# Seven block products in place of eight for the down projection of three MLP quarters, in a two-layer decoder trunk

## The chip, the cores and the metric

One NeuronCore of a Trainium2 chip runs the whole program in one launch. The metric is the device time of one execution in microseconds (us). The engines are TensorE (PE in the profile; PEld is its weight load), VectorE (DVE), ScalarE (ACT), GpSimd (POOL) and SyncE (SP), which issues the DMAs.

## The reference, cut to what matters

Two layers (DEPTH = 2), SEQ = 512 tokens, D_MODEL = 1024, D_FF = 4096, all in float32. Each layer runs four token mixers side by side, merges and projects them, and then runs the MLP, which is the part that is changed:

```python
hm = rms_norm(x, norm_mlp_pre[l])
u = jax.nn.relu(hm @ w_up[l])
x = x + rms_norm(jnp.square(u) @ w_down[l], norm_mlp_post[l])
```

## The kernel before, in words

Activations lie feature-major: 8 tiles of 128 features by 512 tokens. A float32 product is made of three passes of TensorE over rounded parts. Every operand is split into a high part (fp32r) and a low part (the operand minus its high part), and `product3` issues hi·hi, lo·hi and hi·lo into one bank of PSUM. So every weight has to be split: SyncE loads a chunk of 128x1024 values (512 KB), ScalarE writes its high part (`split_ahead`, L1724, or `hi_part`, L1314), and GpSimd writes its low part by a subtraction in four pieces of 128x256 (`lo_pieces`, L1789), which then counts `w_split` up. TensorE waits for `w_split` before it uses the chunk. There are four slots for chunks and four further slots in the slab.

The MLP goes in four quarters of 1024 hidden features (loop variables `q`, `b`). A quarter has 16 units: 8 "up" units (one tile of 128 hidden features each, from 8 contraction steps), then 8 "down" units (one tile of 128 output features each). A unit is 8 contraction steps times 3 passes, 24 matmuls of 128x512 (the first four units of a layer's MLP and its last four go in two halves of 256 tokens). After an up unit ScalarE takes its bank with relu into `tmp` (L1730), and VectorE squares it (L2448), rounds it into `u_hi` (L2450) and subtracts for `u_lo` (L2452). After a down unit VectorE adds its bank to `acc` (L2457), which GpSimd cleared by a memset (L1813). Unit j uses bank 4 + j % 4.

Each engine works through its own queue in program order, and semaphores tie the queues together. In the down units ScalarE and GpSimd split weights three to four chunks ahead of TensorE (`AHEAD` = 3), as the slots come free. Each engine's order is written out by hand in its block; nothing plans it. The squares of the MLP's input, from which its epsilon term comes, are summed by GpSimd in the last quarter.

Of the kernel before, what the change touches and what calls it, by code (L numbers as in the profile page):

```python
# [60 lines left out]
UNITS = MLP0 + 16 * QUARTERS  # L61
# [12 lines left out]
CHUNKS = MLP_CHUNK0 + 16 * QUARTERS  # L74
# [3 lines left out]
SKIPPED = (MLP_CHUNK0 + 10, MLP_CHUNK0 + 13)  # L78
# [5 lines left out]
def slot_of(c):  # L84

    if c < EXTRA:
        return SLOTS + ENTRY.index(c)
    if 0 <= c - MLP_CHUNK0 < EXTRA:
        return SLOTS + c - MLP_CHUNK0
    return (c - 2 - EXTRA * (c > MLP_CHUNK0) + sum(k <= c for k in SKIPPED)) % SLOTS  # L90

# [4 lines left out]
assert (CHUNKS - 2 * EXTRA + len(SKIPPED)) % SLOTS == 0  # L96
# [176 lines left out]
def trunk_kernel(nc, x_in, wproj, wmerge, wrest, par_in, con_in, mask_in, rope_in, out):  # L273
# [5 lines left out]
    with ctx:  # L279
# [35 lines left out]
        def wload(s_):  # L315
# [17 lines left out]
             for i, n in enumerate(("hi", "lo"))]  # L333
        con = sb("con", [P, NCON])
# [14 lines left out]
        ps = [ctx.enter_context(nc.psum_tensor(f"bank{i}", [P, 512], f32)) for i in range(8)]  # L349

# [74 lines left out]
        w_arrived = [ctx.enter_context(nc.semaphore(f"weights_arrived_{s}")) for s in range(SLOTS + EXTRA)]  # L425
        par_loaded = signal("params_loaded", 32)
# [5 lines left out]
        w_split = signal("weights_split", CHUNKS)  # L432
        act_took = signal("act_took_dense", ACT0)
        dve_took = signal("dve_took_dense", DVE0 + 16 * QUARTERS)
        relu_done = signal("relu_ready", 8 * QUARTERS)
        hid_hi = signal("hidden_hi_ready", 8 * QUARTERS)
        dve_step = signal("dve_step", 176)
# [11 lines left out]
        xsummed = signal("x_squares_added", KT - 1)  # L449
# [112 lines left out]
        acc0 = signal("acc_cleared", 1)  # L562
        u_ready = signal("hidden_ready", 8 * QUARTERS)
# [6 lines left out]
        def _(sp):  # L570
# [31 lines left out]
            for layer in layers():  # L602
# [22 lines left out]
                for j in range(EXTRA, 16):  # L625
                    sp.wait_ge(*dense_done.at(layer, FREED_BY[BEFORE[MLP_CHUNK0 + j]] + 1))
                    load(MLP_CHUNK0 + j, rows(wrest, NREST, KT + j))
                more = layer + 1 < LAYERS
                if more:
                    sp.wait_ge(*dense_done.at(layer, MLP0 + EXTRA))  # L630
                    for c in ENTRY:
                        load(c, rows(wproj, NPROJ, NPROJ + c))
                with sp.Fori(0, QUARTERS - 1) as q:
                    for j in range(16):
                        need = sp.snap(layer * UNITS + q * 16 + (MLP0 + 16 + j - SLOTS + 1))
                        sp.wait_ge(dense_done.handle, need)
                        load(MLP_CHUNK0 + 16 + j, wrest[bass.ds(sp.snap(layer * NREST + q * 16 + (KT + 16 + j)), 1)])
# [11 lines left out]
        def _(pe):  # L649
# [5 lines left out]
            for L in layers():  # L655
# [550 lines left out]
                def unit(q, b, j, k, src, cols=slice(0, T)):  # L1206
                    return product3(ps[4 + j % 4][:, cols], weights(MLP_CHUNK0 + 16 * b + j, k), [v[:, k, cols] for v in src],
                                    k == 0, k == KT - 1)
# [3 lines left out]
                def ready(q, b, j):  # L1212
                    more_split = min(max(j - 8, 0), EXTRA) if more and b == QUARTERS - 1 else 0
                    pe.wait_ge(*w_split.at(L, q * 16 + (MLP_CHUNK0 + 16 * b + j + 1 + more_split)))
                    pe.wait_ge(*dve_took.at(L, q * 16 + (DVE0 + 16 * b + j - 3)))

                def units(q, b, times, j0, j1):

                    for j in range(j0, j1):
                        ready(q, b, j)  # L1220
                        for k in range(KT):
                            if j == 8:
                                pe.wait_ge(*u_ready.at(L, q * 8 + (8 * b + k + 1)))
                            ins = unit(q, b, j, k, hn if j < 8 else u)
                        ins.then_inc(*dense_done.up(times))

                for n in range(2):
                    for pair in range(2):
                        if n == 0:
                            pe.wait_ge(*w_split.at(L, MLP_CHUNK0 + 2 * pair + 2))  # L1230
                        for k in range(KT):
                            if pair == 0:
                                pe.wait_ge(*h_ready.at(L, (2 + n) * KT + k + 1))
                            for j in (2 * pair, 2 * pair + 1):
                                ins = unit(0, 0, j, k, hn, HALF[n])
                                if n == 1 and k == KT - 1:
                                    ins.then_inc(*dense_done.up())
# [5 lines left out]
                units(0, 0, 1, 4, 16)  # L1243
                with pe.Fori(0, QUARTERS - 2) as q:
                    units(q, 1, QUARTERS - 2, 0, 16)
                last = QUARTERS - 1
                units(0, last, 1, 0, 11)
                pe.wait_ge(*xsummed.at(L, KT - 1))
                mm(ps[1][:, :], C("ones"), xsq[:, 0, :]).then_inc(*sumsq.up())
                units(0, last, 1, 11, 12)  # L1250
                for n in range(2):
                    for j in range(12, 16):
                        if n == 0:
                            ready(0, last, j)
                        else:
                            pe.wait_ge(*down_half_took.at(L, j - 11))
                        for k in range(KT):
                            ins = unit(0, last, j, k, u, HALF[n])
# [8 lines left out]
        def _(act):  # L1267
# [42 lines left out]
            for L in layers():  # L1310
# [365 lines left out]
                def enter_mlp(n, m0, m1):  # L1676
                    for m in range(m0, m1):
                        act.wait_ge(*x_tiles.at(L, (2 + n) * KT + m + 1))
                        split_x(m, n, hn[0], "mpre")
# [32 lines left out]
                def square(m, n=None):  # L1712

                    cols = slice(0, T) if n is None else HALF[n]
                    act.wait_ge(*(down_half_took.at(L, m - 3) if n == 0 else dve_took.at(L, DVE0 + 16 * (QUARTERS - 1) + 8 + m + 1)))
# [4 lines left out]
                def split_ahead(q, b, j, times):  # L1720
                    c = MLP_CHUNK0 + 16 * b + j + AHEAD
                    s_ = SLOT[c]
                    act.wait_ge(w_arrived[s_], L * (16 * LOADS[s_]) + q * 64 + 16 * LOADED[c])
                    fn(wchunk(0, s_), wload(s_), ACT.Copy).then_inc(*w_hi_done.up(times))  # L1724

                def relu(q, b, j, times):
                    act.wait_ge(*dense_done.at(L, q * 16 + (MLP0 + 16 * b + j + 1)))
                    if j >= 4:
                        act.wait_ge(*u_ready.at(L, q * KT + (8 * b + j - 3)))
                    fn(tmp[:, j % 4, :], ps[4 + j % 4][:, :], ACT.Relu).then_inc(*relu_done.up(times))  # L1730

                for j in range(16):
                    if j == 7:
                        relu(0, 0, j, 1)
                    if j:
                        split_ahead(0, 0, j, 1)
                    if j < 7:
                        relu(0, 0, j, 1)
                with act.Fori(0, QUARTERS - 2) as q:
                    for j in range(16):  # L1740
                        split_ahead(q, 1, j, QUARTERS - 2)
                        if j < 8:
                            relu(q, 1, j, QUARTERS - 2)
# [8 lines left out]
                for j in range(13):  # L1752
                    split_ahead(0, last, j, 1)
# [4 lines left out]
                    if j < 8:  # L1758
                        relu(0, last, j, 1)
# [23 lines left out]
        def _(pool):  # L1783
            pool.memset(v1st[:, :, :], 0.0).then_inc(cleared, 1)
            for L in layers():
# [25 lines left out]
                pool.wait_ge(*m_split.at(L, KT))  # L1811
                pool.sem_inc(carrier, 1)
                pool.memset(acc[:, :, :], 0.0).then_inc(*acc0.up())  # L1813

                def lo_ahead(q, b, j, times):
                    pool.wait_ge(*w_hi_done.at(L, q * 16 + (MLP_CHUNK0 + 16 * b + j + AHEAD + 2)))
                    lo_pieces(SLOT[(MLP_CHUNK0 + 16 * b + j + AHEAD + 1)]).then_inc(*w_split.up(times))

                for j in range(16):
                    lo_ahead(0, 0, j, 1)  # L1820
                with pool.Fori(0, QUARTERS - 2) as q:
                    for j in range(16):
                        lo_ahead(q, 1, j, QUARTERS - 2)
                more = L + 1 < LAYERS

                def lo_in_turn(turn, c):
                    pool.wait_ge(*w_hi_done.at(L, MLP_CHUNK0 + 16 * (QUARTERS - 1) + turn + 1))
                    lo_pieces(SLOT[c]).then_inc(*w_split.up())

                for j in range(16):  # L1830
# [3 lines left out]
                    if i < 16:  # L1834
                        lo_in_turn(i + (min(max(i - 8, 0), EXTRA) if more else 0), MLP_CHUNK0 + 16 * (QUARTERS - 1) + i)
                    if 8 <= i < 12 and more:
                        lo_in_turn(2 * i - 7, CHUNKS + ENTRY[i - 8])
                    if j < KT - 1:
                        if j:
                            pool.wait_ge(*xsummed.at(L, j))  # L1840
                        pool.tensor_tensor(xsq[:, 0, :], xsq[:, 0, :], xsq[:, j + 1, :], ADD).then_inc(*xsummed.up())

        @block.vector
        def _(dve):
# [34 lines left out]
            for L in layers():  # L1879
# [561 lines left out]
                dve.wait_ge(*acc0.at(L, 1))  # L2441
                carry_wait()

                def hidden(q, b, m, times):

                    r_ = tmp[:, m % 4, :]
                    dve.wait_ge(*relu_done.at(L, q * KT + (8 * b + m + 1)))
                    tt(r_, ps[4 + m % 4][:, :], r_, MUL).then_inc(*dve_took.up(times))  # L2448
                    dve.wait_ge(*dve_took.at(L, q * 16 + (DVE0 + 16 * b + m + 1)))
                    dve.tensor_copy(u[0][:, m, :], r_).then_inc(*hid_hi.up(times))  # L2450
                    dve.wait_ge(*hid_hi.at(L, q * KT + (8 * b + m + 1)))
                    tt(u[1][:, m, :], r_, u[0][:, m, :].bitcast(f32), SUB).then_inc(*u_ready.up(times))  # L2452

                def added_down(q, b, m, times):
# [125 lines left out]
```

## Time and profile before

| what | value |
|---|---|
| runs shown | 1925.84 us median of 3 (1922.8 to 1928.35) |
| the profiled execution | 1926.18 us, span 1924.4 us |
| mean granted TensorE clock | 0.994 |
| HBM read over the span | 155.39 MB |
| one MLP (layer 0), without its ends | about 605 to 950 us of the span |

The span is the time from the first to the last instruction on the core. The busy time of TensorE counts a matmul until its modelled end, while the next one has already begun; so the time that a matmul costs is the distance between two starts, not its own length. For VectorE, ScalarE and GpSimd the length of one instruction is close to what it costs, and it includes the time that the instruction stood waiting for a port.

### The profile page before, as it was taken

The page shows a single profiled execution, that of the slowest core. Times are in us where ns is not written, and L with a number is a line of the kernel's source. Part 1 is how long each engine was busy: PE and PEld are TensorE (multiplying, and loading weights), DVE is VectorE, ACT ScalarE, POOL GpSimd, SP SyncE. Part 2 cuts the span into 40 slices and gives each one's busy share as a digit, 9 for nine tenths or more (in the row PEclk, how much of TensorE's full clock was granted, in tenths as well). Part 3 has the DMA queues.
Part 4 walks back from the last instruction along what each step waited for, and adds up shares of the span by engine and source line. Part 5 has one row for each costly group of instructions (what it writes and reads, how often), then busy time and mean ns, then how long its engine had stood idle before and what let it go on. Part 6 is the DMA issues. An engine that isn't in the chain of part 4 may idle for free.

```text
span 1924.4 us, 32405 instructions
## 1 busy us (share of the span) xinstructions
PE 1891.5 (98%) x13030; PEld 1542.4 (80%) x13030; DVE 975.7 (51%) x1779; ACT 775.2 (40%) x1223; POOL 975.4 (51%) x1195
## 2 busy tenths in 40 slices
PE   9999999999999999999999999999999999999997
PEld 8886867778779888888998777678777898888887
DVE  7957987233435422314588579862434362313154
ACT  7544373235536222223474344722354462222223
POOL 3644524326484655557636444353364845555572
PEclk9999999999999999999999999999999999999999
DMA  5222311112131142222203123111122312222222
GB/s 193 80 88 66 99 44 56 36 56 85 59 134 64 66 153 99 98 95 93 97 30 111 66 77 99 45 43 37 52 92 61 136 45 99 99 98 92 94 99 77
DMA packets 52842, 159.44 MB, mean 83 GB/s; under 512 B 5216, under 2 KB 17632, under 8 KB 52448
## 3 DMA queue, kind: packets, MB, share of 16 engines
q1 hardware_dynamic: 51552, 154.65, 23.9%
q10 hardware_dynamic: 1152, 2.86, 0.4%
q8 instruction: 97, 1.59, 0.3%
q14 instruction: 41, 0.34, 0.1%
HBM read 155.39 MB, written 2.10 MB: 82 GB/s over the span
## 4 chain that ended last, share of the span: by engine, by line
PE 88%; DVE 5%; POOL 3%; ACT 3%; issue 1%; DMA 0%; SPq 0%; DVEq 0%; ACTq 0%
PE bank L660 26%; PE bank L662 24%; PE bank L661 24%; POOL w_lo L1789 2%; PE bank L770 1%; PE bank L1039 1%; PE bank L799 1%; PE bank L999 1%; PE bank L785 1%; PE bank L1051 1%; PE bank L862 1%; POOL wx_lo L1789 1%; POOL slab L1810 1%; DVE slab L2215 1%; PE bank L937 1%
## 5 line engine op out<-in xcount | busy, mean ns | idle before, releaser
L1789 POOL TENSOR_TENSOR w_lo<-w_raw,w_hi 128x256 fp32r<-128x256 f32 x1072 | 837.4, 814 | 916.5 <-ACT w_hi L1314 613.4
L660 PE MATMUL bank<-hn_hi,w_hi 128*128 128x512 f32 x1248 | 513.7, 412 | 0.5 <-DVE tmp L1941 0.3
L662 PE MATMUL bank<-hn_hi,w_lo 128*128 128x512 f32 x1248 | 489.2, 392 | 0.5 <-issue 0.5
L661 PE MATMUL bank<-hn_lo,w_hi 128*128 128x512 f32 x1248 | 489.0, 392 | 0.0
L660 PEld LDWEIGHTS bank<-hn_hi,w_hi 128*128 128x128 f32 x1248 | 235.4, 189 | 68.1 <-issue 20.7
L660 PE MATMUL bank<-u_hi,w_hi 128*128 128x512 f32 (+1 forms) x800 | 287.1, 359 | 1.5 <-DVE u_lo L1952 1.1
L1724 ACT ACTIVATE w_hi<-w_raw 128x1024 fp32r<-128x1024 f32 x120 | 127.4, 1061 | 389.8 <-DMA w_raw<-wrest 389.8
L661 PE MATMUL bank<-u_lo,w_hi 128*128 128x512 f32 (+1 forms) x800 | 284.1, 355 | 0.0
L662 PE MATMUL bank<-u_hi,w_lo 128*128 128x512 f32 (+1 forms) x800 | 284.1, 355 | 0.0
L662 PEld LDWEIGHTS bank<-hn_hi,w_lo 128*128 128x128 f32 x1248 | 235.5, 189 | 51.6 <-issue 1.0
L661 PEld LDWEIGHTS bank<-hn_lo,w_hi 128*128 128x128 f32 x1248 | 236.0, 189 | 47.2 <-issue 4.8
L660 PEld LDWEIGHTS bank<-u_hi,w_hi 128*128 128x128 f32 x800 | 151.0, 189 | 26.8 <-DVE u_lo L1952 2.9
L661 PEld LDWEIGHTS bank<-u_lo,w_hi 128*128 128x128 f32 x800 | 151.1, 189 | 21.5 <-issue 0.5
L662 PEld LDWEIGHTS bank<-u_hi,w_lo 128*128 128x128 f32 x800 | 151.0, 189 | 21.3
L1314 ACT ACTIVATE w_hi<-w_raw 128x1024 fp32r<-128x1024 f32 x148 | 155.5, 1056 | 21.5 <-DMA w_raw<-wmerge 12.9
L2457 DVE TENSOR_TENSOR slab<-slab,bank 128x512 f32<-128x512 f32 x56 | 38.5, 688 | 241.5 <-PE bank L662 241.5
L2448 DVE TENSOR_TENSOR tmp<-bank,tmp 128x512 f32<-128x512 f32 x64 | 44.2, 691 | 181.6 <-ACT tmp L1730 181.6
L1374 ACT ACTIVATE tmp<-bank 128x512 f32<-128x512 f32 x64 | 37.5, 602 | 122.4 <-PE bank L662 122.3
L1810 POOL TENSOR_TENSOR slab<-slab,tmp 128x512 f32<-128x512 f32 x48 | 67.7, 1438 | 3.9 <-DVE tmp L1941 3.9
L1730 ACT ACTIVATE tmp<-bank 128x512 f32<-128x512 f32 x64 | 38.4, 599 | 74.2 <-PE bank L662 74.1
L2452 DVE TENSOR_TENSOR u_lo<-tmp,u_hi 128x512 fp32r<-128x512 f32 x64 | 61.4, 959 | 2.2
L2171 DVE CUSTOM_DVE_ANT_0 slab<-bank,slab 128x256 f32<-128x256 f32 (+3 forms) x56 | 28.4, 517 | 61.2 <-PE bank L777 47.1
(405 smaller groups left out, 2877.0 us busy)
## 6 DMA issues: line engine op xcount, KB each, us to landing
w_raw<-wrest SPq DMA_DIRECT2D x136, 512.0 KB, 3.2
w_raw<-wmerge SPq DMA_DIRECT2D x80, 512.0 KB, 3.5
w_raw<-wproj SPq DMA_DIRECT2D x52, 512.0 KB, 3.2
wx_raw<-wproj SPq DMA_DIRECT2D x4, 512.0 KB, 4.8
wy_raw<-wproj SPq DMA_DIRECT2D x4, 512.0 KB, 7.8
slab<-rope ACTq DMA_DIRECT2D x2, 1024.0 KB, 6.0
wx_raw<-wrest SPq DMA_DIRECT2D x4, 512.0 KB, 5.1
wy_raw<-wrest SPq DMA_DIRECT2D x4, 512.0 KB, 5.6
```

The source lines that it names most:

```text
L660: mm(o_, stat[0], mov[0], start=first, stop=False)
L661: mm(o_, stat[0], mov[1], start=False, stop=False)
L662: return mm(o_, stat[1], mov[0], start=False, stop=last)
L1314: fn(wchunk(0, SLOT[c]), wload(SLOT[c]), ACT.Copy).then_inc(*w_hi_done.up(times))
L1374: ins = fn(tmp[:, i % 4, :], b_, ACT.Sigmoid)
L1724: fn(wchunk(0, s_), wload(s_), ACT.Copy).then_inc(*w_hi_done.up(times))
L1730: fn(tmp[:, j % 4, :], ps[4 + j % 4][:, :], ACT.Relu).then_inc(*relu_done.up(times))
L1789: ins = pool.tensor_tensor(wchunk(1, s_)[:, cs], wload(s_)[:, cs], wchunk(0, s_)[:, cs].bitcast(f32), SUB)
L1810: pool.tensor_tensor(acc[:, m, :], acc[:, m, :], tmp[:, m % 4, :], ADD).then_inc(*merged.up())
L2448: tt(r_, ps[4 + m % 4][:, :], r_, MUL).then_inc(*dve_took.up(times))
L2452: tt(u[1][:, m, :], r_, u[0][:, m, :].bitcast(f32), SUB).then_inc(*u_ready.up(times))
L2457: tt(acc[:, m, :], acc[:, m, :], ps[4 + m % 4][:, :], ADD).then_inc(*dve_took.up(times))
```

## The change

Three of the four quarters of each MLP (q = 0, 1, 2) compute their down projection with Strassen's algorithm. The 1024x1024 block of `w_down` is taken as 2x2 blocks of 512x512 (b11 to b22), the hidden features as two halves of 512 features by two halves of 256 tokens, and seven block products take the place of eight.

- TensorE: each product has two units of 24 matmuls of 128x256, so 14 units follow the 8 up units in a quarter, in the order of `TURN` = 3, 6, 5, 7, 4, 1, 2. Products 1 and 6 stay in banks 0 to 3 over the three quarters; the others go through banks 4 to 7 and are taken out after each.
- SyncE: ten of the 14 weight chunks are sums or differences of two blocks, so each comes with two loads of 512 KB (`load_block`), the second into one of three buffers in the slab. The MLP uses six slots in turn here.
- VectorE: it makes the weights' sums (`weights_sum`, 128x1024), the sums of token parts (`tokens_sum`, 128x1024, five in a quarter), the low parts of the seven token parts (`tokens_lo`, 128x1024) and, for the four chunks of products 5 and 2, which have no sum, the weights' low parts (`weights_lo`, 128x1024). It copies or adds the five products that are not kept (`evicted`, two banks each, 128x512). In these quarters the square is written to `u_raw` and is not split. In the last quarter it combines the products into `acc` (`combine`).
- ScalarE: high parts of 14 chunks and of seven token parts (128x1024 each).
- GpSimd: low parts of the 8 up chunks and of 10 of the 14 down chunks, in pieces as before. The memset of `acc` goes, and the sums of the input's squares move to VectorE, at the start of the MLP.
- The last quarter keeps its eight down units. All loops over quarters are unrolled.

The diff, cut to its core:

```diff
+SEVEN, RUN = QUARTERS - 1, KT + 14
+LASTQ = SEVEN * RUN
+FACTORS = {1: ("b11", "b22", "+"), 2: ("b11",), 3: ("b12", "b22", "-"), 4: ("b21", "b11", "-"), 5: ("b22",),
+           6: ("b11", "b12", "+"), 7: ("b21", "b22", "+")}
+TURN = (3, 6, 5, 7, 4, 1, 2)
+BANKS_OF = {3: (4, 5), 6: (2, 3), 5: (6, 7), 7: (4, 5), 4: (6, 7), 1: (0, 1), 2: (4, 5)}
+BY_VECTOR = (5, 2)
...
+    if p < EXTRA:
+        return SLOTS + p
+    if p < 2 * EXTRA:
+        return p - EXTRA
+    if p < LASTQ:
+        return (SLOTS + 2, SLOTS + 3, 0, 1, 2, 3)[(p - 2 * EXTRA) % 6]
...
 # SyncE
+                for p in range(EXTRA, MLP_UNITS):
+                    c = MLP_CHUNK0 + p
+                    sp.wait_ge(*dense_done.at(layer, FREED_BY[BEFORE[c]] + 1))
+                    if rest_row(p) is not None:
+                        load(c, rows(wrest, NREST, rest_row(p)))
+                    else:
+                        load_block(wload(SLOT[c]), p, 0).then_inc(w_arrived[SLOT[c]], 16)
+                    n = sums_to(p)
+                    if n:
+                        i = (n - 1) % 3
+                        if n > 3:
+                            sp.wait_ge(*w_sum.at(layer, n - 3))
...
+                        load_block(second[i][:, :], p, 1).then_inc(second_arrived[i].handle, 16)
...
 # TensorE
+                def seven_products(q):
+
+                    for k, i in enumerate(TURN):
+                        pe.wait_ge(*t_ready.at(L, parts_ready(q, k)))
+                        tokens_ = comb[(7 * q + k) % 3]
+                        for h in range(2):
+                            p = RUN * q + KT + 2 * k + h
+                            if i not in BY_VECTOR:
+                                pe.wait_ge(*w_split.at(L, MLP_CHUNK0 + split_to_count(p)))
...
+                            for d in range(2):
+                                for f in range(4):
+                                    ins = product3(ps[BANKS_OF[i][h]][:, HALF[d]], weights(MLP_CHUNK0 + p, 4 * d + f),
+                                                   [v[:, f, :] for v in tokens_[0:2]],
...
+                            ins.then_inc(*dense_done.up())
...
 # ScalarE
+                for q in range(SEVEN):
+                    for r in range(RUN):
+                        k = (r - KT) // 2
+                        if r == 4:
+                            tokens_hi(q, 0)
+                            tokens_hi(q, 1)
+                        if r >= KT and r % 2 == 0 and k + 2 < 7:
+                            tokens_hi(q, k + 2)
+                        if (q, r) == (0, 0):
+                            split_mlp(4)
+                        if r < KT:
+                            relu(q, r)
+                        if (q, r) != (0, 0) and RUN * q + r + 4 < LASTQ + 3:
+                            split_mlp(RUN * q + r + 4)
...
 # GpSimd
-                pool.memset(acc[:, :, :], 0.0).then_inc(*acc0.up())
...
+                for p in range(EXTRA, LASTQ + EXTRA):
+                    if not split_by_vector(p):
+                        lo_part(MLP_CHUNK0 + p)
...
 # VectorE
+                dve.wait_ge(*mlp_sq.at(L, 2 * KT))
+                for n in (4, 2, 1):
+                    link(tt(xsq[:, 0:n, :], xsq[:, 0:n, :], xsq[:, n:2 * n, :], ADD), xsummed)
...
+                def weights_sum(p):
...
+                    tt(wload(s_), wload(s_), second[i][:, :], ADD if sign == "+" else SUB).then_inc(*w_sum.up())
...
+                    for m in range(KT):
+                        if m == 0 and q:
+                            evicted(q - 1, 6)
+                        squared(q, m)
+                        if m == 3:
+                            tokens_sum(q, 1)
+                            tokens_lo(q, 0)
+                        if m == 4:
+                            weights_sum(RUN * q + m + 4)
+                            tokens_lo(q, 1)
+                        elif m > 4:
+                            weights_sum(RUN * q + m + 4)
+                        if (q, m) == (0, KT - 1):
+                            eps_term()
+                    for k in range(7):
+                        if k + 2 < 7:
+                            tokens_sum(q, k + 2)
+                        weights_sum(RUN * q + KT + 2 * k + 4)
+                        if k:
+                            evicted(q, k - 1)
+                        if k + 2 < 7:
+                            tokens_lo(q, k + 2)
+                        weights_sum(RUN * q + KT + 2 * k + 5)
+                        for h in range(2):
+                            weights_lo(RUN * q + KT + 2 * k + 4 + h)
+                evicted(SEVEN - 1, 6)
...
+                for m in range(KT):
+                    hidden(m)
+                    if m < 3:
+                        combine(m)
+                for m in range(4):
+                    added_down(m)
```

## Rows read from the trace of the kernel before

**Rows 1.** The page: busy time and share of the span; then the chain that ended last

```profile
PE 1891.5 (98%) x13030; PEld 1542.4 (80%) x13030; DVE 975.7 (51%) x1779; ACT 775.2 (40%) x1223; POOL 975.4 (51%) x1195
...
PE 88%; DVE 5%; POOL 3%; ACT 3%; issue 1%; DMA 0%; SPq 0%; DVEq 0%; ACTq 0%
```

**Rows 2.** Windows: first quarter's down units, then the next quarter's up units

```profile
core 0: us, PE busy (x) PEld busy (x) DVE busy (x) ACT busy (x) POOL busy (x), PEclk, DMA share, GB/s
...
651.00:694.50 43.50, 43.50 (x194) 36.03 (x193) 6.63 (x10) 10.16 (x10) 21.13 (x30) 1.00 0.44 157
694.50:738.00 43.50, 43.50 (x194) 36.03 (x193) 16.20 (x22) 12.64 (x15) 25.25 (x36) 1.00 0.29 97
```

**Rows 3.** Windows: a stretch in which all matmuls are 128x256

```profile
597.00:604.90 7.90, 7.90 (x68) 7.90 (x67) 5.74 (x16) 6.16 (x15) 2.44 (x1) 1.00 0.59 195
```

**Rows 4.** Timeline, GpSimd, first quarter's down units: start, length (us), idle before

```profile
655.62 2.83 POOL L1789 TENSOR_TENSOR w_lo<-w_raw,w_hi 128x256 fp32r<-128x256 f32 x4 [8.09 <-ACT w_hi L1724]
```

**Rows 5.** Groups by line and shape: busy, mean ns of one, idle before

```profile
L1789 POOL TENSOR_TENSOR w_lo<-w_raw,w_hi 128x256 fp32r<-128x256 f32 x1072 | 837.4, 814 | 916.5 <-ACT w_hi L1314 613.4 <-ACT w_hi L1724 302.6
...
L2448 DVE TENSOR_TENSOR tmp<-bank,tmp 128x512 f32<-128x512 f32 x64 | 44.2, 691 | 181.6 <-ACT tmp L1730 181.6
...
L2457 DVE TENSOR_TENSOR slab<-slab,bank 128x512 f32<-128x512 f32 x56 | 38.5, 688 | 241.5 <-PE bank L662 241.5
...
L1724 ACT ACTIVATE w_hi<-w_raw 128x1024 fp32r<-128x1024 f32 x120 | 127.4, 1061 | 389.8 <-DMA w_raw<-wrest 389.8
L1730 ACT ACTIVATE tmp<-bank 128x512 f32<-128x512 f32 x64 | 38.4, 599 | 74.2 <-PE bank L662 74.1
```

**Rows 6.** Timeline, VectorE, with GpSimd idle around it

```profile
1243.68 1.23 DVE L2255 TENSOR_TENSOR slab<-slab 128x1024 f32<-128x1024 f32 x1
```

**Rows 7.** Timeline, VectorE, beside a GpSimd that splits weights

```profile
300.02 1.76 DVE L2266 SCALAR_TENSOR_TENSOR slab<-slab 128x1024 f32<-128x1024 f32 x1
301.70 1.76 DVE L2267 TENSOR_TENSOR slab<-slab 128x1024 f32<-128x1024 f32 x1
```

**Rows 8.** Timeline, GpSimd, single pieces in the same stretch

```profile
300.65 1.72 POOL L1789 TENSOR_TENSOR w_lo<-w_raw,w_hi 128x256 fp32r<-128x256 f32 x1
...
302.34 1.72 POOL L1789 TENSOR_TENSOR w_lo<-w_raw,w_hi 128x256 fp32r<-128x256 f32 x1
```

**Rows 9.** Timeline, VectorE then GpSimd, in the last quarter of layer 0

```profile
930.36 9.74 DVE L2479 SCALAR_TENSOR_TENSOR slab<-slab 128x512 f32<-128x512 f32 x1
...
928.65 5.61 POOL L1789 TENSOR_TENSOR w_lo<-w_raw,w_hi 128x256 fp32r<-128x256 f32 x8
```

**Rows 10.** DMA issues: KB each, median us to landing

```profile
w_raw<-wrest SPq DMA_DIRECT2D x136, 512.0 KB, 3.2
```

**Rows 11.** Timeline, TensorE, matmuls after an idle stretch, then windows (PEclk is third from last)

```profile
311.76 0.44 PE L983 MATMUL bank<-con,slab 128*128 128x128 f32 x2 [1.53 <-DVE slab L2282]
...
1265.97 0.90 PE L983 MATMUL bank<-con,slab 128*128 128x128 f32 x3 [3.39 <-DVE slab L2282]
...
312.40:315.80 3.40, 3.37 (x20) 2.97 (x20) 2.56 (x4) 1.33 (x2) 3.40 (x5) 0.50 0.02 5
1264.80:1271.50 6.70, 5.53 (x26) 4.32 (x26) 4.26 (x7) 1.28 (x2) 6.28 (x8) 0.50 0.00 0
```

**Rows 12.** Timeline, VectorE before and at its first square; TensorE, the fifth up unit's start

```profile
621.56 0.48 DVE L1911 SCALAR_TENSOR_TENSOR hn_lo<-x,par,hn_hi 128x256 fp32r<-128x256 f32 x1 [0.18 <-ACT hn_hi L1282]
624.06 0.69 DVE L2448 TENSOR_TENSOR tmp<-bank,tmp 128x512 f32<-128x512 f32 x1 [2.01 <-ACT tmp L1730]
...
629.35 0.40 PE L660 MATMUL bank<-hn_hi,w_hi 128*128 128x512 f32 x1
```

More of the change, by code:

```diff
@@ L333, in trunk_kernel, with at_slab @@
              for i, n in enumerate(("hi", "lo"))]
+        def at_slab(name, shape, unit, dt=f32):
+            return nc.alloc_sbuf_tensor_at(name, shape, dt, offset=slab0 + unit * FT * T * 4)
+        u_raw = at_slab("u_raw", [P, KT, T], 8)
+        comb = [[at_slab(f"comb{i}_{n}", [P, KT // 2, HT], unit + k, dt) for n, k, dt in (("hi", 0, f32r), ("lo", 1, f32r), ("sum", 1, f32))]
+                for i, unit in enumerate((12, 14, 4))]
+        second = [at_slab(f"second{i}", [P, CH], 1 + i) for i in range(3)]
+        g2 = at_slab("g2", [P, KT // 2, HT], 6)
         con = sb("con", [P, NCON])
@@ L633, in _, with load_block @@
[L633 to L637, printed above, removed]
+                def load_block(into, p, which):
+                    q, r = p // RUN, p % RUN - KT
+                    name = FACTORS[TURN[r // 2]][which]
+                    f, d = int(name[1]) - 1, 4 * (int(name[2]) - 1) + 2 * (r % 2)
+                    src = rows(wrest, NREST, KT + 16 * q + KT + d, 2)[:, :, f * 4 * P:(f + 1) * 4 * P]
+                    return sp.dma_start(into.rearrange("p (d n) -> p d n", d=2), src.rearrange("d p n -> p d n"))
@@ new lines, in _ @@
+                for p in range(EXTRA, MLP_UNITS):
[10 more added lines that the diff above has]
+                            sp.wait_ge(*w_sum.at(layer, n - 3))
+                        else:
+                            sp.wait_ge(*xsummed.at(layer, 3))
+                        load_block(second[i][:, :], p, 1).then_inc(second_arrived[i].handle, 16)
+                    if p == LASTQ + EXTRA + 2 and more:
+                        sp.wait_ge(*dve_took.at(layer, took0(SEVEN) + 3))
+                        for c_ in ENTRY:
+                            load(c_, rows(wproj, NPROJ, NPROJ + c_))
@@ L1210, in _, with ready @@
                 more = L + 1 < LAYERS
[L1212 to L1217, printed above, removed]
+                def ready(q, j):
+                    more_split = min(max(j - 8, 0), EXTRA) if more and q == SEVEN else 0
+                    pe.wait_ge(*w_split.at(L, MLP_CHUNK0 + split_to_count(RUN * q + j) + more_split))
+                    pe.wait_ge(*dve_took.at(L, took0(q) + (j - 3 if j >= 4 else (-1, 0, -3, -2)[j])))
@@ L1242, in _ @@
                                 half_sum(0, 1, True, True, tmp[:, 0, :], tmp[:, 2, :], tmp[:, 3, :])
[L1243 to L1248, printed above, removed]
-                mm(ps[1][:, :], C("ones"), xsq[:, 0, :]).then_inc(*sumsq.up())
-                units(0, last, 1, 11, 12)
+                units(0, 4, 7)
+                pe.wait_ge(*xsummed.at(L, 3))
+                mm(ps[1][:, :], C("ones"), xsq[:, 0, :]).then_inc(*sumsq.up())
+                units(0, 7, KT)
+                seven_products(0)
+                for q in range(1, SEVEN):
+                    units(q, 0, KT)
+                    seven_products(q)
+                units(SEVEN, 0, 12)
                 for n in range(2):
@@ L1253, in _ @@
                         if n == 0:
-                            ready(0, last, j)
+                            ready(SEVEN, j)
                         else:
@@ L1257, in _ @@
                         for k in range(KT):
[L1258 removed]
+                            ins = unit(SEVEN, j, k, u, HALF[n])
                             if (n, j, k) == (1, 12, 6):
@@ L1732, in _, with split_mlp @@
[L1732 to L1743, printed above, removed]
+                def split_mlp(p):
+                    c = MLP_CHUNK0 + p
+                    if sums_to(p):
+                        act.wait_ge(*w_sum.at(L, sums_to(p)))
+                        fn(wchunk(0, SLOT[c]), wload(SLOT[c]), ACT.Copy).then_inc(*w_hi_done.up())
+                    else:
+                        hi_part(c)
@@ L2463, in added_half @@
                     tt(acc[:, m, cols], acc[:, m, cols], ps[4 + m % 4][:, cols], ADD)\
                         .then_inc(*(down_half_took if n == 0 else dve_took).up())
-                def quarter(q, b, times, downs):
-                    for m in range(KT):
-                        hidden(q, b, m, times)
-                    for m in range(downs):
-                        added_down(q, b, m, times)
-                quarter(0, 0, 1, KT)
-                with dve.Fori(0, QUARTERS - 2) as q:
-                    quarter(q, 1, QUARTERS - 2, KT)
```

242 lines of the change are left out of this document (166 added, 76 removed).

## The prediction

> **What bounds the kernel now.** I read the page first [rows 1]: TensorE is busy 98% of the span and makes 88% of the chain that ended last; no other engine has more than 51%. The windows over a quarter of the MLP say the same: in 43.5 us of down units TensorE never stops, while VectorE works 6.63 us, ScalarE 10.16 and GpSimd 21.13 [rows 2]. So only fewer or shorter matmuls can shorten the MLP, and only if the helpers, which have so much room, can feed them. What they get to do is the question.
>
> **TensorE's part.** The down window holds 192 matmul starts (194 touch it, two began earlier), 43.5 / 192 = 0.2266 us each, 5.44 us a unit, 43.5 us for eight units [rows 2]. At 128x256 the window has 66 starts in 7.90 us, 0.1197 us each, not half of 0.2266 = 0.1133 [rows 3]. A unit of the new kind is 24 x 0.1197 = 2.87 us and 14 of them take 40.2 us. The quarter saves 3.3 us, not the 5.4 of one unit in eight; six quarters (three in each of two layers) save 19.7 us. The bound from both sides is narrow, since both shapes run here already.
>
> **What the helpers get, per quarter.** GpSimd makes the low part of a chunk in 2.83 us when nothing is in its way [rows 4]; that is already 99% of a new unit's 2.87 us. VectorE's 128x1024 operation with both inputs in SBUF takes 1.23 us alone [rows 6]. A quarter has 10 weights' sums, 5 token sums, 7 token low parts and 4 weights' low parts: 26 of them, 32 us, plus 8 squares of 0.69 and 10 evictions of 0.69 (both read PSUM) [rows 5], 12.4 us. ScalarE has 22 + 7 copies of 1.06 and 8 relus of 0.60 [rows 5], 35.5 us of 83.7: it has room.
>
> **They get in each other's way.** Beside a GpSimd that splits weights, two such operations of VectorE start 1.68 us apart (300.02 and 301.70) and last 1.76 [rows 7], and the pieces of GpSimd between them start 1.69 us apart (300.65 and 302.34) and last 1.72, where a free one costs 2.83 / 4 = 0.71 [rows 8, 4]. So the two alternate: one operation of 1.23 and one piece of 0.71 cost 1.68 together, hardly less than their sum, 1.94. Over the whole kernel the mean piece is 814 ns for that reason [rows 5]. Operations of VectorE that read PSUM keep 0.69 [rows 5].
>
> The Trainium skill (SBUF — State Buffer, section SBUF: two separate sides) calls the pair of ports an exclusive lock that is held for the whole instruction, also against a VectorE operation with two SBUF inputs. The trace agrees in kind, and not quite in size: by the rule as written a pair would cost 1.94, by the rows 1.68. With the some 13 pairs of a quarter that stand below in front of TensorE the rule would add 13 x 0.26 = 3.4 us per quarter, some 20 us in all, and the time would be 1993 (an estimate). I go by the rows.
>
> **Does the work fit?** Over a whole quarter it does: 72 pieces of GpSimd, 26 of them in pairs at 1.68 and 46 at 0.71, are 76 us of 83.7. But not in the stretch of the products. There, with t = 0 at the end of the last up unit, GpSimd has to deliver chunks 14 to 19 (products 7, 4, 1; I number by unit in the quarter), all of them sums, for units that start at t = 17.2, 20.1, 23.0, 25.8, 28.7 and 31.6. It can't be far ahead: a chunk is loaded only when the unit six before it is done, and the sum comes first. I walk through VectorE's order by the durations above.
>
> - t = 0.7 to 4: square of tile 7, sum for chunk 11, token sum for product 5. ScalarE's copies behind them (chunk 11, tokens, 12, 13) end at 7.1.
> - 5 to 9.6: token low part, low parts of chunks 12 and 13, paired with the pieces of chunk 11, which is ready at 8.5 (needed at 8.6). Product 5 starts in time, at 11.5.
> - 9.6 to 12.1: token sum for 7, then the sum for chunk 14. ScalarE has its high part at 13.2. GpSimd stood idle from 8.5 to here.
> - From 13.2 GpSimd has always work, and VectorE has nearly always some of the same kind: low tokens of 7, sums 15 and 16, low tokens of 4, sum 17, token sum 1, sum 18, low tokens of 1, sum 19, token sum 2, low tokens of 2, low parts 20 and 21. Thirteen operations, each followed by one piece. Chunk 14 is ready at 18.9 (three pairs), 1.7 late; 15 at 25.7 (four pairs), TensorE then has waited 3.9 more; 16 at 30.4, 1.8 more (two pairs, two pieces beside evictions); 17 at 35.2, 1.9; 18 at 40.0, 1.8. After that VectorE waits for TensorE, and GpSimd makes chunk 19 at 2.83 in time.
>
> The sum is 11.1 us of waiting in a product stretch, which becomes 51.3 us. A cross-check: 24 pieces from 13.2 to 42.8 are 13 x 1.68 + 11 x 0.71 = 29.6. The extremes: with no pairing 24 x 0.71 = 17 us, from 13.2 to 30.2, and no wait (bound 0); with all pairs at 1.94, 14 to 15 us. GpSimd's backlog then (the next quarter's up chunks 22 to 25) is made at 2.83 beside units of 5.44 and is worked off there, with the sums of chunks 8 to 11: no wait.
>
> **The rest, at nothing.** The memset of `acc` and the sums of squares leave GpSimd where it has room [rows 2]; on VectorE they stand between 622.0 and 624.1, and some 4.3 us of sums (2048, 1024 and 512 values: 2.3 + 1.23 + 0.69, an estimate by the length in rows 6) push the first square to 626.3, while unit 4, which needs its bank, starts at 629.35 [rows 12]. If that cover is gone it costs up to 2 us a layer. `combine` (5 of 1.23 and 6 of 0.69, 10 us) lies in three up units of 5.44 beside `hidden` (2.2 to 2.8 each), some 3 us late, behind four banks. Loads: 3.2 us each [rows 10], 32 in a quarter in place of 16; at 43.5 us the first quarter moved 157 GB/s at a DMA share of 0.44 [rows 2], the stretch of products has 24 x 0.52 MB in 51 us, some 250 GB/s. A sum's loads start at the latest five units (14 us) ahead: cost 0, up to 2 us per quarter if they take twice as long. The clock: a wait of TensorE of 1.53 us and one of 3.39 were each followed by or fell in a stretch at half clock (1.2 GHz), 3.4 and 6.7 us long [rows 11]. Five waits of 1.7 to 3.9 us per quarter invite it. While GpSimd is the bound, a slow unit (5.7 us against the 4.8 us between chunks) costs at most 0.9; behind the last wait it costs half its length, 1.7. I take 0, since a dense stream surrounds these waits; the bound is 0 to 3 us per quarter.
>
> **The sum.** 1926.2 (profiled execution: span 1924.4 and 1.8 around it, 0.3 above the median of the runs) - 19.7 + 6 x 11.1 = 1973.1 us; I say 1973.
>
> **Rivals.**
> 1. The helpers keep up (not slower). One mechanism: VectorE is held at its own waits (for a high part, a load, an evicted bank) more than I think, GpSimd runs at 2.83 meanwhile and gets ahead, and the wait per quarter falls under the 3.3 us saved: that is the point from which it decides. For it: the whole quarter fits (76 of 83.7). Against: the order above shows VectorE with ready work nearly throughout, and rows 7 and 8. With 0 to 2 us of wait: 1906.5 to 1918, middle 1912. Chance 0.20.
> 2. Near balance, 2.5 to 4 us of wait per quarter: 1921 to 1930. Chance 0.07.
> 3. Slower still: the half clock behind the waits (+3 per quarter), or VectorE kept from the port. Once in this trace an operation of 0.7 us lasted 9.74 us while GpSimd ran through [rows 9]. One of these per quarter delays the sums by up to 9 us. 6 x 14 to 6 x 17: 1990 to 2009, middle 1995. Chance 0.15.
> 4. The products don't do what they say (TensorE's time per unit not 2.87 but that of a full one): excluded by rows 3.
>
> **How the numbers follow.** The forecast has 0.58 with its own range 1950 to 1990 (7 to 14 us of wait per quarter). The bound for telling a change is 0.3%, 6 us: faster 0.21 (rival 1 and the low end of 2), same 0.06, slower 0.73. The range goes from 1911, in the middle of rival 1, to 1993.
>
> **What would show it.** Right: in the window of a product stretch TensorE is idle some 11 us, its releaser GpSimd's low parts, first before the first unit of product 7 and most before its second; the stretch lasts 51 us; pieces of GpSimd there last over 1 us in the mean, VectorE's 128x1024 operations 1.6; the up units stay at 43.5. Wrong: if waits begin in product 5, VectorE's own chain is the bound; if they end at ScalarE or a DMA, the loads are; if there are none, rival 1 holds. If matmuls of 128x256 start 0.12 us apart the first term holds.

## The result and the profile after

The changed kernel takes 1979.6 us (median of 4 runs, 1977.5 to 1982.2) against 1925.4 us of the kernel before (median of 4): ratio 1.0282, 95% interval 1.0265 to 1.0298. The forecast was 1973 us, slower. The profiled execution has a span of 1980.4 us, 56.0 more than before.

First the page of the changed kernel, the same lines as [rows 1], then its four costliest waits of TensorE (waited for: us in total, times, longest):

```profile
PE 1894.0 (96%) x13894; PEld 1584.0 (80%) x13894; DVE 1142.3 (58%) x1879; ACT 850.9 (43%) x1301; POOL 1090.9 (55%) x1227
...
PE 78%; POOL 9%; DVE 7%; ACT 4%; issue 2%; DMA 1%; SPq 0%; DVEq 0%; ACTq 0%
```

```profile
PE bank L772 <- POOL w_lo L1944: 21.5, 10, 2.6
PE bank L772 <- DVE comb_lo L2626: 17.0, 6, 3.6
PE bank L772 <- issue: 9.3, 6, 2.7
PE bank L772 <- POOL wy_lo L1944: 7.0, 5, 1.7
```

GpSimd has gone from 3% to 9% of the chain. Now windows, cut at the borders between up units and products of the changed kernel: the first product stretch, the up units behind it, and the second and third product stretches. They answer to [rows 2].

```profile
core 0: us, PE busy (x) PEld busy (x) DVE busy (x) ACT busy (x) POOL busy (x), PEclk, DMA share, GB/s
...
653.79:708.10 54.31, 44.41 (x337) 43.55 (x336) 36.08 (x32) 21.23 (x21) 43.43 (x42) 0.94 0.57 193
708.10:751.65 43.55, 43.55 (x194) 36.05 (x193) 12.97 (x14) 13.17 (x16) 22.75 (x31) 1.00 0.44 147
751.65:803.22 51.57, 43.12 (x337) 42.10 (x336) 35.38 (x30) 21.19 (x21) 44.42 (x43) 0.97 0.59 203
...
846.77:899.76 52.99, 44.06 (x338) 43.21 (x337) 34.97 (x30) 19.11 (x19) 41.13 (x38) 0.94 0.52 178
```

The up units are as before, with TensorE busy throughout. All of the loss is in the product stretches: the six last 54.3, 51.6, 53.0, 54.3, 51.6 and 51.6 us, 316.4 together, where eight down units took 43.5, six times that 261.1. The difference is 55.3 of the 56.0 us. In a stretch TensorE stands idle 8.4 to 9.9 us (9.0 in the mean), and the mean granted clock is 0.94 or 0.97.

Where it waits shows in its timeline in the first stretch (start, length, idle before and its releaser); unit 14, the first of product 7, is the one at 674.96:

```profile
674.96 0.36 PE L772 MATMUL bank<-comb_hi,wy_hi 128*128 128x256 f32 x1 [3.59 <-DVE comb_lo L2626]
680.62 0.39 PE L772 MATMUL bank<-comb_hi,wy_hi 128*128 128x256 f32 x1 [1.06 <-POOL wy_lo L1944]
686.45 0.36 PE L772 MATMUL bank<-comb_hi,w_hi 128*128 128x256 f32 x1 [2.70 <-issue]
...
692.11 0.39 PE L772 MATMUL bank<-comb_hi,w_hi 128*128 128x256 f32 x1 [2.55 <-POOL w_lo L1944]
```

And what GpSimd and VectorE do there:

```profile
657.61 4.81 POOL L1944 TENSOR_TENSOR w_lo<-w_raw,w_hi 128x256 fp32r<-128x256 f32 x4 [3.54 <-ACT w_hi L1861]
668.09 12.47 POOL L1944 TENSOR_TENSOR wy_lo<-wy_raw,wy_hi 128x256 fp32r<-128x256 f32 x8 [5.66 <-ACT wy_hi L1861]
680.53 19.84 POOL L1944 TENSOR_TENSOR w_lo<-w_raw,w_hi 128x256 fp32r<-128x256 f32 x20
```

```profile
668.04 1.21 DVE L2626 TENSOR_TENSOR comb_lo<-comb_sum,comb_hi 128x1024 fp32r<-128x1024 f32 x1
669.17 1.76 DVE L2610 TENSOR_TENSOR wy_raw<-wy_raw,second 128x1024 f32<-128x1024 f32 x1
670.85 1.75 DVE L2610 TENSOR_TENSOR w_raw<-w_raw,second 128x1024 f32<-128x1024 f32 x1
...
674.20 1.74 DVE L2610 TENSOR_TENSOR w_raw<-w_raw,second 128x1024 f32<-128x1024 f32 x1
675.86 1.75 DVE L2619 TENSOR_TENSOR comb_sum<-u_raw 128x1024 f32<-128x1024 f32 x1
```

GpSimd is idle for 5.66 us until 668.09, then makes chunks 14 and 15 in 12.47 us, eight pieces of 1.56 in the mean, while two operations of VectorE in a row start 1.68 apart (669.17 and 670.85). The wait at 674.96 is put down to a token low part of VectorE that was done at 669.25. That is the case in which one has to look for another of the awaited semaphores: the fourth of GpSimd's pieces, which ended at 674.86.

### The profile page after: what moved, and what is told of

The parts are those of the page before. It is cut to its first block, busy times and chain, and to the rows that moved or that the text cites. A ratio compares the mean times of both kernels' runs of the same rounds, so it can differ in the third digit from the quotient of the medians.

```text
span 1980.4 us, 33847 instructions
## 1 busy us (share of the span) xinstructions
PE 1894.0 (96%) x13894; PEld 1584.0 (80%) x13894; DVE 1142.3 (58%) x1879; ACT 850.9 (43%) x1301; POOL 1090.9 (55%) x1227
## 4 chain that ended last, share of the span: by engine, by line
PE 78%; POOL 9%; DVE 7%; ACT 4%; issue 2%; DMA 1%; SPq 0%; DVEq 0%; ACTq 0%
PE bank L772 23%; PE bank L773 21%; PE bank L774 21%; POOL w_lo L1944 6%; POOL wy_lo L1944 2%; PE bank L882 1%; PE bank L1151 1%; PE bank L911 1%; PE bank L897 1%; PE bank L1111 1%; PE bank L1163 1%; DVE comb_sum L2619 1%; PE bank L974 1%; DVE slab L2356 1%; PE bank L1049 1%
## 5 line engine op out<-in xcount | busy, mean ns | idle before, releaser
L772 PE MATMUL bank<-comb_hi,w_hi 128*128 128x256 f32 x448 | 133.7, 298 | 39.6 <-POOL w_lo L1944 21.5
L1944 POOL TENSOR_TENSOR wy_lo<-wy_raw,wy_hi 128x256 fp32r<-128x256 f32 x152 | 140.5, 956 | 47.7 <-ACT wy_hi L1451 25.8
L772 PE MATMUL bank<-u_hi,w_hi 128*128 128x256 f32 (+1 forms) x416 | 136.9, 329 | 1.4 <-DVE u_lo L2093 1.1
L773 PE MATMUL bank<-u_lo,w_hi 128*128 128x256 f32 (+1 forms) x416 | 134.8, 324 | 0.0
L774 PE MATMUL bank<-u_hi,w_lo 128*128 128x256 f32 (+1 forms) x416 | 134.7, 324 | 0.0
L773 PE MATMUL bank<-comb_lo,w_hi 128*128 128x256 f32 x448 | 131.3, 293 | 0.0
L774 PE MATMUL bank<-comb_hi,w_lo 128*128 128x256 f32 x448 | 131.1, 293 | 0.0
L772 PEld LDWEIGHTS bank<-comb_hi,w_hi 128*128 128x128 f32 x448 | 90.8, 203 | 43.5 <-POOL w_lo L1944 19.8
L773 PEld LDWEIGHTS bank<-comb_lo,w_hi 128*128 128x128 f32 x448 | 90.9, 203 | 0.2
L774 PEld LDWEIGHTS bank<-comb_hi,w_lo 128*128 128x128 f32 x448 | 90.7, 202 | 0.0
```

Of the source, the lines that this page charges most:

```text
L772: mm(o_, stat[0], mov[0], start=first, stop=False)
L773: mm(o_, stat[0], mov[1], start=False, stop=False)
L774: return mm(o_, stat[1], mov[0], start=False, stop=last)
L1944: ins = pool.tensor_tensor(wchunk(1, s_)[:, cs], wload(s_)[:, cs], wchunk(0, s_)[:, cs].bitcast(f32), SUB)
```

## The experiments

Each kernel is compared with the kernel before, run beside it on the same chip (1925.3, 1924.4 or 1926.6 us). A single run can be off by some 4 us: the 13 runs of the kernel before in the first comparison went from 1921.5 to 1928.8. The chunks are numbered by unit in the quarter, as in the prediction.

**Back to GpSimd.** The one part of the change that its name speaks of, undone:

```diff
-BY_VECTOR = (5, 2)
+BY_VECTOR = ()
```

> The low parts of the four chunks without a sum (products 5 and 2) go back from VectorE to GpSimd; the rest is the changed kernel (1979.6 us). Theory (GpSimd and VectorE take turns at one pair of ports, and GpSimd's low parts come too late for TensorE): GpSimd gets 16 more pieces per product stretch, 11 us at 0.71 each, of which it can hide about 5 in its idle time around chunk 12 and 13; VectorE has 4 operations of 1.23 less. The stretch grows by 2 to 6 us: 1992 to 2015, most likely 2000. Rival (VectorE's own chain of operations in program order is the bound): taking 4 x 1.23 us from it shortens the stretch by up to 5 us: 1950 to 1975.

Measured: 1979.3 us, 1.0276 times before (1.0259 to 1.0293), the same as the changed kernel. Both theories missed. GpSimd's timeline in the first stretch:

```profile
654.30 17.21 POOL L1944 TENSOR_TENSOR w_lo<-w_raw,w_hi 128x256 fp32r<-128x256 f32 x12 [3.54 <-ACT w_hi L1861]
671.47 5.56 POOL L1944 TENSOR_TENSOR wy_lo<-wy_raw,wy_hi 128x256 fp32r<-128x256 f32 x8
676.99 17.03 POOL L1944 TENSOR_TENSOR w_lo<-w_raw,w_hi 128x256 fp32r<-128x256 f32 x16
```

From 654.30 on it has no idle time now: chunks 11 to 13 go through at once. The low parts of VectorE had only filled, on VectorE, the time in which GpSimd then stood idle for chunk 14, whose sum was queued behind them. Chunk 15 is ready 26.6 us into the stretch (677.03, the stretch starts at 650.48), and in the changed kernel 26.8 (680.56, from 653.79). Handing these four chunks over took work from GpSimd where it had a hole. The six stretches last 314.2 us; TensorE waits 47.0 us in them in place of 54.1, but 13 stretches of 3.4 us are at half clock in place of nine. The section on the prediction comes back to this exchange.

**No late low parts by GpSimd.**

```diff
+                        if p < LASTQ and p % RUN >= KT + 6:
...
+                            pool.tensor_tensor(wchunk(1, s_)[:, 0:8], wload(s_)[:, 0:8], wchunk(0, s_)[:, 0:8].bitcast(f32), SUB)\
...
+                                    w_ = [w_[0], w_[0]] if i in (7, 4, 1) else w_
```

> Leaves out work: for the six chunks of products 7, 4 and 1 GpSimd writes 8 columns of the low part in place of 1024, and TensorE uses the high part a second time there. VectorE, ScalarE, the loads and the number of matmuls stay. Theory (supply of low parts by GpSimd, at shared ports): no waits at these units, VectorE's 128x1024 operations there fall to 1.2 us, the stretch is 40 to 42 us, no half clock in it: 1908 to 1914. Rival (VectorE's chain in program order is the bound, GpSimd only looks late): waits of 5 us and more per stretch stay, over 1940.

Measured: 1911.1 us, one run. The second stretch and the up units ahead of it:

```profile
693.00:736.45 43.45, 43.45 (x193) 35.95 (x192) 12.97 (x14) 13.18 (x16) 22.84 (x31) 1.00 0.43 147
736.45:777.30 40.85, 40.67 (x337) 40.41 (x336) 30.64 (x30) 21.02 (x21) 19.13 (x25) 1.00 0.75 256
```

With all of VectorE's operations, all loads (256 GB/s) and all matmuls in place the stretch lasts 40.9 us at full clock. So VectorE's chain, ScalarE and the DMAs could feed TensorE; GpSimd's six chunks and what they do to the others, by turns at the ports and by the clock behind TensorE's waits, are the whole loss.

**No late sums by VectorE.**

```diff
+                    cs = slice(0, CH) if p % RUN < KT + 6 else slice(0, 8)
+                    tt(wload(s_)[:, cs], wload(s_)[:, cs], second[i][:, cs], ADD if sign == "+" else SUB).then_inc(*w_sum.up())
```

> Leaves out work: for the six chunks of products 7, 4 and 1 VectorE adds 8 columns of the second block in place of 1024. GpSimd's pieces stay as they are. Theory (ports are shared, the two add up): six of some 13 pairs per stretch go, each gives GpSimd back about 1 us; the waits fall from 10 to 2 to 4 us per stretch, pieces there fall to about 0.85 us: 1930 to 1945. Rival 1 (GpSimd's own pace of 2.83 us per chunk against 2.87 us per unit is the bound, sharing or not): waits stay at 8 to 10, 1970 to 1980. Rival 2 (VectorE's chain alone): no waits, 1908 to 1914.

Measured: 1949.0 us, one run, 4 us beyond the range of the theory (as much as a single run can be off), and 21 us and more from both rivals. The second stretch, and GpSimd in it:

```profile
743.59:789.41 45.82, 41.42 (x338) 40.56 (x337) 27.70 (x30) 21.02 (x21) 38.85 (x43) 1.00 0.66 228
```

```profile
756.56 7.82 POOL L1944 TENSOR_TENSOR w_lo<-w_raw,w_hi 128x256 fp32r<-128x256 f32 x8 [4.34 <-ACT w_hi L1861]
764.33 8.62 POOL L1944 TENSOR_TENSOR wy_lo<-wy_raw,wy_hi 128x256 fp32r<-128x256 f32 x8
772.91 7.54 POOL L1944 TENSOR_TENSOR w_lo<-w_raw,w_hi 128x256 fp32r<-128x256 f32 x8
```

GpSimd makes the six chunks in 24.0 us, where the changed kernel needs 12.47 for the first two alone. TensorE still waits 4.4 us, and the clock stays full in this stretch (in three of the six 3.4 us are at half clock). GpSimd alone would need 17 (24 pieces of 0.71): its own pace is not the bound, the turns with VectorE are, and fewer of them cost less.

**Ten low parts by VectorE, in another order.** `BY_VECTOR = (5, 7, 4, 1, 2)`, with TensorE waiting for each chunk by itself, and on VectorE:

```diff
+                        if k:
+                            evicted(q, k - 1)
                         if k + 2 < 7:
                             tokens_sum(q, k + 2)
-                        weights_sum(RUN * q + KT + 2 * k + 4)
-                        if k:
-                            evicted(q, k - 1)
+                        for h in range(2):
+                            weights_sum(RUN * q + KT + 2 * k + 4 + h)
                         if k + 2 < 7:
                             tokens_lo(q, k + 2)
-                        weights_sum(RUN * q + KT + 2 * k + 5)
```

> VectorE makes the low parts of all ten chunks of products 5, 7, 4, 1 and 2; GpSimd keeps products 3 and 6 and the up chunks. TensorE waits for each chunk by itself, and VectorE's order per product is: evictions, token sum, both weights' sums, token low part, both low parts. A low part costs VectorE 1.23 us in place of four pieces of GpSimd at 0.71 with a turn of VectorE between them. Theory (shared ports are the bound): the work at the ports per stretch falls, 25 operations of 1.23 and 10 evictions of 0.69 are 37.7 us of 40.2, so the waits fall to 1 to 4 us per stretch: 1915 to 1938, most likely 1925. Rival (VectorE becomes the bound through its own queue and its waits for ScalarE): waits of 8 us or more per stretch, over 1955.

Measured: 1924.1 us, 0.9994 times before (0.9984 to 1.0003): 55 us less than the changed kernel, and level with the one before. The second stretch, and GpSimd in it:

```profile
736.68:779.81 43.13, 41.25 (x337) 40.52 (x336) 37.16 (x36) 20.92 (x21) 11.38 (x14) 1.00 0.72 243
```

```profile
740.50 4.80 POOL L1944 TENSOR_TENSOR wy_lo<-wy_raw,wy_hi 128x256 fp32r<-128x256 f32 x4 [2.63 <-ACT wy_hi L1861]
774.42 6.10 POOL L1944 TENSOR_TENSOR wy_lo<-wy_raw,wy_hi 128x256 fp32r<-128x256 f32 x8 [29.12 <-ACT wy_hi L1451]
```

GpSimd is idle for 29 us of the stretch, VectorE makes more in the same time, and TensorE waits 1.9 us in place of 8.5.

**Shares alone, and order alone.** The first has only the shares and the waits per chunk of the kernel above, the second only the order and the waits per chunk, with `BY_VECTOR = (5, 2)`.

> As e4_ten_low_by_vector (VectorE makes the low parts of products 5, 7, 4, 1 and 2, and TensorE waits per chunk), but VectorE's order stays that of the changed kernel: evictions between the two sums, the second sum behind the token low part. Theory: the work at the ports decides, so most of the 55 us that e4 gained stay: 1925 to 1940; VectorE waits for ScalarE's high part of the second chunk, some 1 us in each of three products. Rival (the order, not the share, made e4 fast): 1955 and more.

> The changed kernel with VectorE's order and TensorE's waits per chunk from e4_ten_low_by_vector, but the shares as they were: VectorE makes the low parts of products 5 and 2 only. With e6 (shares only, 1938.9 us) and e4 (both, 1924.1) it completes the square. Theory (GpSimd's low parts, taken in turns with VectorE's operations, are the bound, so the order on VectorE moves little): 1970 to 1985. Rival (e4 gained by its order, in which evictions don't stand behind sums): 1940 to 1965.

Measured: 1938.9 us (1.0076, 1.0060 to 1.0091) and 1978.3 us (1.0268, 1.0251 to 1.0285), both as the theory had it.

| | shares of the changed kernel | ten low parts by VectorE |
|---|---|---|
| VectorE's old order | 1979.6 | 1938.9 |
| new order | 1978.3 | 1924.1 |

The shares bring 41 us. The order brings 1 while GpSimd is the bound, less than the runs can tell, and 15 once it isn't. In the kernel with shares alone TensorE waits once per stretch, for the evictions of product 5, which stand behind a sum:

```profile
PE bank L772 <- DVE slab L2646: 12.7, 4, 3.2
PE bank L772 <- DVE slab L2644: 7.8, 2, 3.9
```

Behind each of these six waits of 3.2 to 3.9 us lie 3.4 us at half clock, which cost some 1.5 us each. So some 9 of the 15 us that the order brought are clock: in the kernel with both changes no wait in a product stretch is longer than 1.5 us, and no product stretch has any half clock.

**One piece in place of four.** The changed kernel, with `pool.tensor_tensor(wchunk(1, s_), wload(s_), wchunk(0, s_).bitcast(f32), SUB)` for the down chunks.

> The changed kernel with GpSimd's low part of each down chunk as one operation of 128x1024 in place of four of 128x256. Theory (what counts is the sum of the work at the shared ports, not who gets the next turn): the sum stays, a chunk gets through at once but VectorE's sums for the next ones wait up to 2.8 us longer; waits per stretch change by at most 2 us: 1967 to 1992. Rival (GpSimd is late because VectorE cuts in after each piece): with no turn of VectorE inside a chunk the waits halve or go: 1925 to 1955.

Measured: 1959.5 us, one run: between the two ranges. From its groups by shape, and from GpSimd's timeline:

```profile
L2614 DVE TENSOR_TENSOR w_raw<-w_raw,second 128x1024 f32<-128x1024 f32 x40 | 75.6, 1893 | 0.0
```

```profile
764.50 2.39 POOL L1970 TENSOR_TENSOR w_lo<-w_raw,w_hi 128x1024 fp32r<-128x1024 f32 x1 [2.26 <-ACT w_hi L1861]
766.84 3.39 POOL L1970 TENSOR_TENSOR wy_lo<-wy_raw,wy_hi 128x1024 fp32r<-128x1024 f32 x1
```

A chunk takes 2.39 us alone and 3.39 with a turn of VectorE, where four pieces with four turns take 6.7; VectorE's sums last 1893 ns in the mean (1483 in the changed kernel). Work moved up for GpSimd and back for VectorE, and TensorE's largest wait was then 4.3 us per stretch at the evictions of product 5. The forecast of this run fell, and with it the premise that the sum of the work stays: a chunk costs GpSimd 2.39 us in place of 2.83, which over six late chunks in six stretches is 16 us (an estimate) of the 20 gained. So it isn't shown that who gets the next turn counts; it may be the smaller sum alone.

**Eleven low parts by VectorE, holes filled.**

```diff
+ORDER_DVE = ("ts2", "wl11", "tl2", "wl12", "wl13", "ep0", "ev0", "ts3", "ws14", "ws15", "tl3", "wl14", "wl15", "ws16", "tl4", "wl16", "ev2",
+             "ws17", "ts5", "wl17", "ws18", "tl5", "wl18", "ws19", "ts6", "wl19", "ev3", "tl6", "wl20", "wl21", "ev4")
...
+                    for o in ORDER_DVE:
```

Here ts and tl are a product's token sum and low part, ws and wl a chunk's sum and low part, ev a product's evictions, ep the epsilon term.

> VectorE makes the low parts of 11 chunks (also the second one of product 6, in the 1.2 us in which it stood waiting for ScalarE), and its order is written out so that each low part has another operation between it and its sum, and the evictions of product 5 come before product 4 needs the banks. Theory (in e4 VectorE's queue is the bound by 1 to 2.5 us per stretch, GpSimd idle for 29 us of it): the waits fall to 0 to 1 us per stretch, the stretch to 40.7 to 41.7 us: 1908 to 1916. Rival (loads, 24 of 512 KB in a stretch, come too late once nothing else waits): TensorE's waits stay over 2 us with VectorE's sums waiting for a DMA, 1918 to 1926.

Measured: 1913.8 us (5 runs, 1912.3 to 1916.8), 0.9946 times before, 0.9932 to 0.9959. It is the fastest of the kernels that leave no work out, and faster than the kernel before by 0.5%. Its second stretch and its first:

```profile
740.75:781.72 40.97, 40.59 (x338) 40.41 (x336) 37.77 (x37) 21.02 (x21) 7.79 (x10) 1.00 0.77 255
654.91:697.21 42.30, 41.20 (x338) 40.53 (x337) 39.06 (x39) 20.91 (x21) 6.89 (x9) 1.00 0.73 246
```

TensorE waits 0.4 and 1.1 us; the six stretches last 248.7 us, 12.4 less than 48 down units took before.

## Why the prediction was right

- *TensorE's part, 40.2 us per stretch, 19.7 us saved.* Right. Without GpSimd's late low parts the last of the six stretches has no wait and lasts 40.45 us, 0.2 more than 336 x 0.1197; the other five are 40.7 without their waits of 0.2 to 0.7. So the six quarters can save some 17 rather than 19.7; the kernel with eleven low parts by VectorE gets 12 of them.
- *The two take turns, one pair 1.68 us.* Right: VectorE's operations start 1.68 apart beside GpSimd (669.17, 670.85). Taking away either partner removes the waits (GpSimd, to 0.2 us in the second stretch) or halves them (VectorE's sums, 8.5 to 4.4). Of the Trainium skill's exclusive lock (SBUF — State Buffer, SBUF: two separate sides) the rows again show the turns, and again a pair at 1.68 and not the full sum.
- *Waits of 11.1 us per stretch at chunks 14 to 18.* 8.4 to 9.9 measured. The second stretch follows the walk closely: units 17 and 18 start 35.2 and 40.0 us into it (786.82 and 791.63), as worked out, and the stretch lasts 51.6 for 51.3. In the first, the wait came at chunk 14, as said, but was 3.6 us and not 1.7, since GpSimd began 1.1 us later than in my walk (668.09, 14.3 us into the stretch) and all of its four pieces were paired; those behind were 1.1, 2.7 and 2.6 us, and chunk 18 was not waited for. So the sign that most of the wait would stand before product 7's second unit failed there. The 1.1 us are the epsilon term, which VectorE makes in the first quarter ahead of its token sum and which the walk left out:

```profile
656.36 0.68 DVE L2652 TENSOR_SCALAR slab<-bank 128x512 f32<-128x512 f32 x1
657.08 0.69 DVE L2653 SCALAR_TENSOR_TENSOR slab<-slab 128x512 f32<-128x512 f32 x1
```

- *The clock, taken as 0.* This term was too small, though less so than it looks. The two stretches of half clock behind the waits of the first product stretch:

```profile
675.30:678.70 3.40, 3.40 (x19) 3.40 (x18) 3.40 (x3) 2.11 (x2) 3.40 (x3) 0.50 0.54 203
692.40:695.80 3.40, 3.40 (x18) 3.40 (x18) 0.00 (x0) 1.06 (x1) 3.40 (x6) 0.50 0.03 13
```

  There are nine of 3.4 us in the six stretches. In them matmuls start 0.21 us apart in place of 0.12:

```profile
676.08 0.41 PE L772 MATMUL bank<-comb_hi,wy_hi 128*128 128x256 f32 x1
676.29 0.41 PE L773 MATMUL bank<-comb_lo,wy_hi 128*128 128x256 f32 x1
```

  Each costs TensorE some 1.55 us, 14 in all, 2.3 per stretch; my bound was 3. I had argued that a dense stream around the waits would keep the clock up. Waits of 2.5 to 3.6 us lowered it, though not each time, and in the two fastest of the kernels that leave no work out, whose longest wait in a product stretch is 1.5 us, no product stretch has any. But six of the nine lie ahead of a further wait for GpSimd, whose pieces run on without a gap (668.09 to 700.37 in the first stretch), so what they cost is taken off that wait: unit 14 lasts 1.6 us longer, and unit 15 waits 1.06 us for its chunk in place of some 2.6. Only the three behind the last wait of a stretch (692.4 in the first, one each in the third and the fourth) lengthen it, by 1.4 to 1.6 us, 4.6 in all or 0.8 per stretch. These stretches last 54.3, 53.0 and 54.3 us, the other three 51.6. The prediction had this exchange, small cost while GpSimd is the bound and 1.7 behind the last wait, and then took 0. It is argued from the rows; no run keeps the clock up.
- *The sum.* 51.3 us per stretch forecast, 52.7 measured. In TensorE's time the waits are 2.1 less, the clock 2.3 more, and its own part 1.2 more (52.7 - 9.0 - 2.3 = 41.4 for 40.2; in the units around a wait a few matmuls are slower). That the first two nearly cancel isn't luck, since most of the slow clock stands where TensorE would have waited: 0.8 by the clock, 0.4 by the two first stretches, which ran late, and 0.2 by which the others exceed the walk is the plainer account. 6 x 1.4 = 8 us lead from 1973 to 1981; the profiled execution took 1982.2, the median 1979.6.
- *The chosen chunks.* The prediction didn't ask what the four chunks at VectorE brought by themselves. They brought nothing (1979.3 us without), because they were those for which GpSimd had time.
- *Loads, `combine`, sums of squares at nothing.* Loads right: 256 GB/s at a DMA share of 0.75 in the second stretch of the kernel without GpSimd's late low parts. The one matmul of the epsilon term moved from the last quarter to the first, with its 0.9 us; apart from it the first quarter's up units take what they took (47.0 us for 46.1), and the last quarter's, with `combine` beside them, 43.5. So both cost nothing.

Still open is how much of the 20 us of the one-piece kernel is GpSimd's shorter total (2.39 for 2.83) and how much the turns, and why the pieces of chunks 16 and 17 took some 2 us longer in the first stretch than in the second.

## What to carry to other kernels

Compute what two engines that take turns at a port need together, and for the busiest stretch, not for the whole loop: here 76 of 84 us fitted over a quarter, and TensorE still waited 9 inside it. If both are full, give the work to the engine that needs the port for less time per element (1.13 us per 128x1024 on VectorE against 2.83 on GpSimd, or 6.7 for four turns with four operations of VectorE in them), even if that one is the busier. After that fill the holes of its own queue, in which it waits for its partner of the pipeline; before that the order was worth nothing here that the runs can tell.

## What the runs showed of the hardware

- VectorE's 128x1024 operations on two SBUF inputs follow each other at 1.13 to 1.15 us where neither GpSimd nor a wait is in the way, less than the 1.22 that each lasts; I had summed 1.23. In the kernel with eleven low parts by VectorE:

```profile
742.19 1.22 DVE L2615 TENSOR_TENSOR wy_raw<-wy_raw,second 128x1024 f32<-128x1024 f32 x1
743.32 1.22 DVE L2624 TENSOR_TENSOR comb_sum<-u_raw 128x1024 f32<-128x1024 f32 x1
```

- GpSimd's subtraction of 128x1024 took 2.39 us as one instruction and 2.83 as four, so each further piece costs some 0.15 us.
- In the product stretches of the changed kernel TensorE waited 2.5 us and more eleven times, and eight of these waits had 3.4 us at half clock (1.2 GHz) behind them; a wait of 2.71 us had none, and one of 2.45 had. So a wait's length alone doesn't tell. In the kernel with shares alone each wait of 3.2 to 3.9 us had 3.4 us, and in the one-piece kernel the one of 4.3 us in each stretch had 6.8. In the kernel without late sums two of five waits of 2.6 us had none.
